# Second block of a two-block transformer on one core: the memory is loaded into idle tiles and scaled among the columns, its split is one stretch, and its units follow at once

## The reference

```python
def second_block(...):
    h = x
    for l in range(DEPTH):                    # DEPTH = 2
        u = rms_norm(h, g_mix_pre[l])
        if l % 2 == 0:
            u = mlstm_rglru_mixer(u, ...)     # layer 0
        else:
            u = sliding_window_sink_attention(u, ...)   # layer 1
        h = h + rms_norm(u, g_mix_post[l])
        u = memory_cross_attention(rms_norm(h, g_x_pre[l]), mem, g_mem[l], ...)
        h = h + rms_norm(u, g_x_post[l])
        u = squared_relu_mlp(rms_norm(h, g_ff_pre[l]), w_ff1[l], w_ff2[l])
        h = h + rms_norm(u, g_ff_post[l])
    return h

def memory_cross_attention(u, mem, g_mem, w_q, w_kv, w_o):
    q = (u @ w_q).reshape(B, S, X_HEADS, X_HD)
    kv = (rms_norm(mem, g_mem) @ w_kv).reshape(B, M, 2, X_HEADS, X_HD)
    k, v = kv[:, :, 0], kv[:, :, 1]
    s = jnp.einsum('bshd,bmhd->bhsm', q, k) * (X_HD ** -0.5)
    p = jax.nn.softmax(s, axis=-1)
    o = jnp.einsum('bhsm,bmhd->bshd', p, v).reshape(B, S, D_MODEL)
    return o @ w_o
```

## Time and profile before

| | |
|---|---|
| median of 3 runs | 3508.6 us (3507.53 to 3509.79) |
| profiled execution | 3509.08 us, span 3507.3 us, 1.8 us around it |
| mean granted clock of TensorE | 0.991 |
| busy: PE, DVE, ACT | 3372.8, 1792.9, 1329.5 us |
| chain that ended last | PE 76%, DVE 13%, ACT 7% |

### The profile page before, as it was taken

One profiled execution on the slowest core, in us unless ns is written; L12 is line 12 of the kernel. 1 busy time (PEld: TensorE's weight loads), 2 busy tenths in 40 slices (PEclk: granted clock), 3 DMA queues, 4 the chain that ended last, 5 costly groups with the idle time before them and its releaser, 6 DMA issues.

```text
span 3507.3 us, 38141 instructions
## 1 busy us (share of the span) xinstructions
PE 3372.8 (96%) x15592; PEld 2760.8 (79%) x15592; DVE 1792.9 (51%) x2722; ACT 1329.5 (38%) x2106; POOL 62.1 (2%) x64
## 2 busy tenths in 40 slices
PE   8999989999999999899999999999999989999998
PEld 6888767888878887678888778777888778778886
DVE  4333685533463337854334765546444665655444
ACT  3222554322242225543322554334322565434321
POOL 0000100000000000000000000000000000000000
PEclk9999999999999999999999999999999999999999
DMA  4332311333333323114333233212333313213332
GB/s 149 98 98 89 83 49 54 103 96 96 96 90 97 96 86 83 49 49 119 98 96 96 66 102 97 82 57 75 102 96 99 82 55 96 67 52 111 96 96 66
DMA packets 604286, 304.10 MB, mean 87 GB/s; under 512 B 43600, under 2 KB 601808, under 8 KB 603984
## 3 DMA queue, kind: packets, MB, share of 16 engines
q1 hardware_dynamic: 604112, 301.66, 30.1%
HBM read 299.52 MB, written 2.10 MB: 86 GB/s over the span
## 4 chain that ended last, share of the span: by engine, by line
PE 76%; DVE 13%; ACT 7%; issue 2%; DMA 1%; SPq 0%; DVEq 0%; ACTq 0%
PE ps L1637 24%; PE ps L1638 23%; PE ps L1645 23%; DVE wl L2033 2%; DVE tmp L2042 1%; DVE Y L2202 1%; ACT wh L1816 1%; DVE XR L2125 1%; ACT XH L1860 1%; PE ps L1801 1%; PE ps L1785 1%; DVE XL L2111 1%; ACT tmp L1887 1%; PE ps L1702 1%; PE ps L1668 1%
## 5 line engine op out<-in xcount | busy, mean ns | idle before, releaser
L1637 PE MATMUL ps<-XH,wh 128*128 128x512 f32 x2600 | 1046.4, 402 | 37.2 <-DVE wl L2033 15.1
L1645 PE MATMUL ps<-XL,wh 128*128 128x512 f32 (+1 forms) x2856 | 1059.8, 382 | 0.0
L1638 PE MATMUL ps<-XH,wl 128*128 128x512 f32 x2600 | 1018.6, 392 | 0.0
L2033 DVE TENSOR_TENSOR wl<-raw,wh 128x1024 fp32r<-128x1024 f32 (+1 forms) x565 | 680.3, 1209 | 528.8 <-ACT wh L1816 528.4
L1816 ACT ACTIVATE wh<-raw 128x1024 fp32r<-128x1024 f32 (+1 forms) x565 | 584.2, 1039 | 553.3 <-PE ps L1645 485.7
L1645 PEld LDWEIGHTS ps<-XL,wh 128*128 128x128 f32 x2856 | 539.9, 189 | 105.1
L1637 PEld LDWEIGHTS ps<-XH,wh 128*128 128x128 f32 x2600 | 491.9, 189 | 157.3 <-DVE wl L2033 30.1
L1638 PEld LDWEIGHTS ps<-XH,wl 128*128 128x128 f32 x2600 | 492.3, 189 | 100.5 <-issue 3.1
L1637 PE MATMUL ps<-HHa,wh 128*128 128x512 f32 x1088 | 428.9, 394 | 14.8 <-DVE HLa L2037 11.4
L1638 PE MATMUL ps<-HHa,wl 128*128 128x512 f32 x1088 | 423.9, 390 | 0.0
L1645 PE MATMUL ps<-HLa,wh 128*128 128x512 f32 x1088 | 408.1, 389 | 0.0
(11 more groups left out here) (324 smaller groups left out, 3099.0 us busy)
## 6 DMA issues: line engine op xcount, KB each, us to landing
raw<-in_ffn_w_gu SPq DMA_DIRECT2D x176, 512.0 KB, 3.8
raw<-in_w_ff SPq DMA_DIRECT2D x128, 512.0 KB, 4.1
raw<-in_ffn_w_down SPq DMA_DIRECT2D x64, 512.0 KB, 3.9
raw<-in_w_xkv SPq DMA_DIRECT2D x32, 512.0 KB, 3.9
raw<-in_ev_w_in SPq DMA_DIRECT2D x25, 512.0 KB, 3.9
raw<-in_ffn_w_down SPq DMA_DIRECT2D x32, 384.0 KB, 3.3
raw<-in_w_in SPq DMA_DIRECT2D x24, 512.0 KB, 3.9
raw<-in_w_out SPq DMA_DIRECT2D x64, 128.0 KB, 2.7
```

What stands on the lines that cost most here:

```text
L1637: e.matmul(bank[:, 0:n], t.wh[u % SPL][:, k, :], h, start=first, stop=False)
L1638: e.matmul(bank[:, 0:n], t.wl[u % SPL][:, k, :], h, start=False, stop=False)
L1645: m = e.matmul(bank[:, 0:n], t.wh[u % SPL][:, k, :], l, start=False, stop=last)
L2033: self.e.tensor_tensor(wl, raw, f32(wh), ALU.subtract).then_inc(self.s["lo"], self.tag("lo", f"lo.{i}"))
```

## The change

The change has three parts.

(a) In the first layer the memory is loaded early into a new tile HX, which lies over tiles of HHa that are idle then, ahead of the RG-LRU weights. It is scaled in 3, 3 and 2 instructions behind the o projections of heads 0, 1 and 2, and split in one stretch behind that of head 3, before the o gate's sigmoid and the head's last rest. HHa is released for later use only when the split is done.

(b) In the job loop unit n stands in job n, for n from 0 to 15.

(c) In the second layer the scaling goes in 3, 3 and 2 behind queries 4, 5 and 6, the parts take 3 filler steps rather than 9, the filler takes a step each 1.5 ticks during the units (EVERY_MEM), and DELAY2 is 8 rather than 4.

```diff
--- before.py
+++ after.py
@@ -37,8 +37,9 @@
 
 EVERY1 = 2.8
 EVERY2 = 2
+EVERY_MEM = 1.5
 DELAY1 = 8
-DELAY2 = 4
+DELAY2 = 8
 
 C_ID = 0
 C_ONE = 128
@@ -155,6 +156,8 @@
         self.XM = sb("XM", [P, KD, T])
         self.XL = sb("XL", [P, KD, T], F32R)
         self.Y = sb("Y", [P, KD, T])
+        with nc.sbuf_tensor("HX", [P, 4, T], F32) as HX:
+            self.HX = HX
         self.HHa = sb("HHa", [P, KD, T], F32R)
         self.HLa = sb("HLa", [P, KD, T], F32R)
         with nc.sbuf_tensor("HHb", [P, KD, T], F32R) as HHb, nc.sbuf_tensor("HLb", [P, KD, T], F32R) as HLb:
@@ -991,6 +994,9 @@
         rr, rrt = self.pre_scale(nxt)
         kk = self.uid("mx2")
 
+        mem = Memory(self, 0, t.HX[:, :, :], [self.hid_free[s] for s in range(4)])
+        mem_normed = mem.normed()
+
         gb, gt = nxt()
         G, f = self.tmp.take()
         self.p_gate_in(f"{kk}.g", G, gb, rr, (gt, f, rrt))
@@ -1123,17 +1129,23 @@
             ob, ot = nxt()
             to = self.mul(M1[:, 4 + h, :], ob[:, :], rr[:, :], ot, menter, rrt)
             self.psum.give(ob, to)
+            for _ in range(3):
+                next(mem_normed, None)
+            if h == 3:
+                self.x_used(ot)
+                for _ in mem.parts():
+                    pass
+                for s in range(4):
+                    self.hid_free[s] = [self.hid_free[s], mem.raw_done]
             for _ in rest:
                 pass
             k = self.uid("o")
             self.p_sigmoid_own(k, M1[:, 4 + h, :], to)
             tv = v_rest()
             qkvo.append((tq, tk, tv, k))
-        self.x_used(ot)
         self.tmp.give(rr, to)
         self.tmp.give(rw, lru_state[3])
         self.tmp.give(rx, lru_state[3])
-        mem = Memory(self, 0, t.XM[:, 4:8, :], self.x_free)
 
         extra = [Y[:, i, :] for i in (0, 1, 4, 5)]
         self.lend(extra, self.y_free)
@@ -1187,13 +1199,6 @@
                 return r
             return rest
 
-        def memory_parts():
-            yield from mem.normed()
-            yield from mem.parts()
-
-        prep = memory_parts()
-
-        MEM2 = {n: (n - 5,) if n < 17 else (2 * n - 22, 2 * n - 21) for n in range(5, 19)}
         jobs = [(h, s) for h in range(4) for s in range(NB)]
         late = []
         SKEW = 3
@@ -1202,10 +1207,8 @@
                 weights_of(*jobs[n])
             if late:
                 r = late.pop()()
-            for _ in range(4):
-                next(prep, None)
-            for i in MEM2.get(n, ()):
-                mem.unit(i)
+            if n < 16:
+                mem.unit(n)
             if n >= SKEW:
                 h, s = jobs[n - SKEW]
                 td = products(h, s)
@@ -1295,11 +1299,12 @@
         self.tmp.give(rr, vts[1])
         for i in range(4, 8):
             query(i)
-            if i == 4:
-                for _ in mem.normed():
-                    pass
-        for _ in mem.parts():
-            next(self.filler[0], None)
+            for _ in range(3):
+                next(mem_normed, None)
+        for n, _ in enumerate(mem.parts()):
+            if n % 3 == 2:
+                next(self.filler[0], None)
+        self.filler[1] = EVERY_MEM
         for i in range(16):
             mem.unit(i)
 
```

## The result

The changed kernel took 3519.8 us (median of 7 runs, 3517.5 to 3522.0) against 3508.6 of the kernel before, a ratio of 1.0029 with a 95% interval of 1.002 to 1.0039 (the ratio isn't exactly the quotient of the two medians): 10 to 11 us slower. The forecast was 3504 us, a gain of 5, with a range up to 3515. The profiled execution has a span of 3515.7 us against 3507.3; it is the fastest of its 7.

A forecast was written before the change was run, and what follows sets the result against it. TensorE, busy 96% of the span, was taken as the bound, so only its waits and slow clock could be won. First layer 8.0 us gained less second layer 3.0 lost gave 5.0, hence 3504 us, range 3494 to 3515.

The forecast's parts named there:

- First layer, the gain: First layer's jobs, last projection column to output projection: removed waits and lost clock cut 96.1 to 86.9 us, 9.2 gained.
- First layer, the cost: Before the first layer's jobs: three scalings behind head 0 delay the convolution, 1.25 us lost; early memory load counted at nothing.
- rival D: First layer: load delays RG-LRU weights 3.4 us, grown wait lowers the clock, about 1.6 us; total 3509 us, chance 0.11.
- Delay 8 in place of 4 ... I net the two to nothing: Second layer's attention start: first rope wait (4.6 us) shrinks, but the first turn waits for normalisation; net zero.
- Second layer, up to unit 0: Second layer's queries: exponentials ahead of rope lengthen the head loop from 10.29 to 11.4 us, 1.2 more for queries 4 to 6.
- Then unit 0: Second layer's first memory unit: ends at 2862 with 28 steps done, against 2870.45 with 35; 8.4 us earlier.
- The one wait of 6 us ahead of it: Second layer's parts, before the first memory unit: TensorE waits 6 us for a copy behind exponentials, rope and 2 parts.
- The units: Second layer's memory units: heads take 8.9 us on the mean against TensorE's 8.1; 8 us of new waits, counted as 4.8.
- six tenths: Second layer's memory units: share of the 8 us of serial waits counted, 4.8 us, since TensorE gets splits up to four units ahead.
- rival C: Second layer's units: a second split in every head, 9.85 us a head, 17.5 us lost; 7.7 us slower, 3516, chance 0.15.
- 6.6 us of steps put off: Second layer: 7 attention steps not done before the first memory unit, 0.95 us each, return in the units.
- the sum for the second layer: Whole second layer: 1.8 us gained up to the first memory unit, 4.8 lost in the units; 3.0 us lost.

The follow-up runs named there:

- first layer alone: Changed kernel with DELAY2 4, no EVERY_MEM rate, and the second layer's scaling and parts steps as before: 3502.5 us, 0.9980 of the kernel before.
- delay 7: Changed kernel with DELAY2 7 rather than 8: 3515.6 us, 1.0016 of the kernel before.
- delay 4: Changed kernel with DELAY2 4 rather than 8: 3501.9 us, 0.9978 of the kernel before.
- delay 10: Changed kernel with DELAY2 10 rather than 8: 3506.0 us, 0.9991 of the kernel before.
- late exponentials: Changed kernel, DELAY2 still 8, with last maximum and exponentials issued at the start of the next step: 3529.3 us, 1.0054 of the kernel before.

## Why the prediction was wrong

- **First layer, the gain: right.** 9.2 us forecast, 96.10 - 86.65 = 9.45 measured in the jobs. The clock stayed at 1.00 and the first products met no wait.
- **First layer, the cost: right in size and in cause.** 1.25 us forecast; from group 0's matmuls to group 1's it is 29.84 us against 28.67, 1.17 more, and moving the scalings away gave it back. The load ahead of the weights cost nothing, as counted, but not by 0.4 us of cover: it delayed the weights by 2.3 and 1.8 us, where I had allowed up to 3.4, and the later of them landed 2.9 us ahead. So the first half of rival D is out. Its second half, a clock that falls after the grown wait, came true at times: in two of the ten traces with scalings behind head 0 (first layer alone, wait 2.74 us, and delay 7, 2.71) the clock was at half for 3.4 us there, and the way from group 1 to the jobs took 90.9 us instead of 89.3, the 1.6 us of D. Behind the jobs up to 1.5 us were in no term.
- **"Delay 8 in place of 4 ... I net the two to nothing": half right and beside the point.** The first wait (4.59 us) fell away and a first wait at the transposes of 3.17 us came instead. What mattered was the next term.
- **The failed step is the query loop in "Second layer, up to unit 0".** I had seen that the exponentials come directly ahead of the rotary phase, and summed a loop of 11.4 us, 12.6 with scalings. Measured: 12.15, 14.99, 15.78 and 13.00. The sum took the last 3.4 us, scores and norms, as work that VectorE does without waiting. But TensorE had been blocked at the transposes until then, and its fourth score comes only behind two more slices of query work: VectorE waited 0.77, 2.43, 2.96 and 0.82 us for it. With this wait, and none, three, three and two scalings of 0.42 us, the sum gives 12.2, 15.1, 15.6 and 13.1. I had two engines in the loop, and it has three. And I had TensorE at full clock there: the two long waits are the two with the clock at half, and without that they would be about 0.8 us too, to judge by the other two heads. In the runs, delay 4 against 8 with all else equal is worth 12 us (in the kernels with only the first layer's change) and 16 to 18 (in the changed kernel, 11.5 of it in the queries and 3.5 in the units). I had 3.3 for the loop.
- **Then unit 0:** forecast 8.4 us earlier relative to the start of the stretch, measured 1.7, so 6.7 us of the miss lie up to here. The one wait of 6 us ahead of it was right (5.59, for a copy on ScalarE).
- **The units: right before I discounted them.** The serial sum gave 8.9 us a head; measured 9.98 and 7.84 in turn, mean 8.9. I took six tenths of the excess on the ground that TensorE is handed splits up to four units ahead. The trace shows no such relief. The value units are longer still (8.73 and 10.53, mean 9.6), which only rival C had a term for. From unit 0 to the end I had 6.6 us of steps put off and 4.8 of waits, 11.4 us, and measured 18.6 - 0.6 = 18.0: another 6.6 us of the miss, 3.2 of them the discount. So the sum for the second layer, 3.0 us lost, measured 751.3 - 735.0 = 16.3. But what the rate can win back is smaller than the units look: 16.2 us of the units are 3 to 5 us of time, since steps put off must run later.
- **The rivals.** The sign was that of C, and its place was half right: it put all of the loss in the units, and its mean of 9.85 us a head was not reached. The range ended at 3515, just under C's 3516, the largest price that I allowed for the second layer, and none of the rivals priced a longer query loop. That C's time came within 4 us of the measured one is luck: it paid for the units alone.

## What to carry to other kernels

A filler that interleaves two streams has a phase as well as a rate. Before its delay is changed, write down for each engine what of the other stream stands between a head's last maximum and the first copies that TensorE needs; if it is a long block, every head pays for it. In a loop over three in-order engines, a block on one doesn't add its length once: the engine that was held up has its own queue to work off, for which the first then waits. And a serial sum that reproduces a measured loop (10.3 and 10.29) deserves to be used in full. Last, to see what an edit costs at a place, compare the time between two fixed points and not only the wait: the wait depends also on when the waiting engine comes.

## What the runs showed of the hardware

TensorE's clock fell to the half level in the queries though no single wait there but the first (3.17 us) was over 2.3 us: 0.67 in 2815 to 2820, after waits of 1.33 and 2.21 us at 2810.92 and 2814.27, with TensorE busy 1.87 us in the 5 us before. The kernel with delay 4 had waits of up to 1.8 us in the window shown, the closest 4 us apart, and 1.00. The kernel with delay 10 had pairs of waits of 1.2 to 1.6 us, 3 us apart, in its queries, and stayed at 1.00 too. In the kernel with late exponentials, with single waits of 3.4 to 4.6 us, the mean was 0.86 over 2774 to 2860. Nor does one wait's length decide alone: behind RG-LRU group 1 the clock fell after 2.71 and 2.74 us and not after 2.69 or less. What exactly the clock asks for, these runs don't show.

A load of 1 MB issued 0.6 us ahead on the same queue delayed the landing of two loads of 256 KB by 2.3 and 1.8 us (7.1 and 6.7 us against 4.8 and 4.9).
